# Streaming hybrid-attention step on one core: in the attention loop TensorE weighs the values of an older unit before it multiplies the next unit's scores

## What is computed

```python
s = einsum('bqkgd,bskd->bkgqs', q * d ** -0.5, k)       # scores
s = where(ok, s - slope[h] * distance, -inf)            # ALiBi and mask
p = softmax(concatenate([s, s_meta, sink], -1), -1)     # the sink in A alone
out = einsum('bkgqs,bskd->bqkgd', p, v)                 # weighs the values
```

## Time and profile before

| | |
|---|---|
| median of 3 runs | 1902.87 us (1902.35 to 1903.76) |
| the profiled execution | 1903.1 us |
| its span, first to last instruction | 1901.3 us |
| around the span | 1.8 us |
| granted TensorE clock | 0.998 of full speed |
| PE busy | 1879.1 us, 99% |
| PEld busy | 1778.6 us, 94% |
| DVE busy | 1136.7 us, 60% |
| ACT busy | 712.9 us, 37% |
| POOL busy | 611.2 us, 32% |

### The profile page before, as it was taken

How to read it: one execution, slowest core, us unless ns; L and a number is a source line. 1 busy time by engine, 2 the same in 40 slices (tenths; PEclk the granted TensorE clock), 3 DMA queues, 4 the chain that set the end, 5 groups by cost and what they waited for, 6 DMA issues and landing times.

```text
span 1901.3 us, 32833 instructions
## 1 busy us (share of the span) xinstructions
PE 1879.1 (99%) x11892; PEld 1778.6 (94%) x11892; DVE 1136.7 (60%) x2694; ACT 712.9 (37%) x1424; POOL 611.2 (32%) x493
## 2 busy tenths in 40 slices
PE   9999999999999999999999999999999999999997
PEld 8899999877778999999998889999999999999996
DVE  5259999999765667676664553333333333333336
ACT  5345554233345556555673442222222222222222
POOL 4225554134344334444341022222222222222223
PEclk9999999999999999999999999999999999999999
DMA  6433333233556444444323331111111111111114
GB/s 205 116 84 85 99 95 94 83 107 91 124 134 144 102 102 102 102 102 91 68 69 126 114 126 45 45 44 44 44 44 44 44 44 44 44 44 44 44 44 144
DMA packets 180398, 160.26 MB, mean 84 GB/s; under 512 B 101472, under 2 KB 148432, under 8 KB 180288
## 3 DMA queue, kind: packets, MB, share of 16 engines
q1 hardware_dynamic: 164816, 139.72, 25.9%
q10 hardware_dynamic: 15472, 19.09, 4.4%
HBM read 120.63 MB, written 39.27 MB: 84 GB/s over the span
## 4 chain that ended last, share of the span: by engine, by line
PE 93%; DVE 2%; DMA 0%; issue 0%; SPq 0%; ACT 0%; DVEq 0%
PE ps L1084 23%; PE ps L1906 20%; PE ps L2472 19%; PE ps L1806 11%; PE ps L1782 6%; PE ps L1764 5%; PE ps L2153 5%; PE ps L1056 2%; PE ps L2134 0%; PE ps L2000 0%; DVE y L2416 0%; PE ps L1111 0%; DVE probs L1692 0%; DMA m_in<-merged_scr 0%; DVE total L2396 0%
## 5 line engine op out<-in xcount | busy, mean ns | idle before, releaser
L2472 PE MATMUL ps<-hid_hi,weights 128*128 128x362 f32 (+1 forms) x1536 | 380.3, 327 | 0.0
L1906 PE MATMUL ps<-x2T_hi,weights 128*128 128x362 f32 (+1 forms) x1536 | 378.0, 326 | 0.0
L1906 PEld LDWEIGHTS ps<-x2T_hi,weights 128*128 128x128 f32 x1536 | 272.1, 188 | 0.1
L2396 DVE TENSOR_TENSOR total<-total,ps 128x362 f32<-128x362 f32 (+1 forms) x360 | 189.2, 532 | 138.5 <-PE ps L2472 138.5
L2472 PEld LDWEIGHTS ps<-hid_hi,weights 128*128 128x128 f32 x1536 | 270.4, 188 | 0.0
L1906 PE MATMUL ps<-x2T_lo,weights 128*128 128x362 f32 (+1 forms) x768 | 251.4, 327 | 0.0
L2472 PE MATMUL ps<-hid_lo,weights 128*128 128x362 f32 (+1 forms) x768 | 250.2, 326 | 0.0
L1084 PE MATMUL ps<-xT_hi,w 128*128 128x362 f32 (+1 forms) x960 | 246.1, 330 | 1.6 <-PEq L181 1.6
L2381 DVE TENSOR_TENSOR hidden<-hidden 128x362 f32<-128x362 f32 (+1 forms) x96 | 51.5, 537 | 293.5 <-ACT hidden L2356 293.5
L1893 POOL TENSOR_TENSOR weights<-down_raw,weights 128x512 fp32r<-128x512 f32 x64 | 83.8, 1312 | 380.6 <-ACT weights L1887 380.6
L1035 DVE MATCH_REPLACE8 score<-top,score 128x1024 f32<-128x1024 f32 (+5 forms) x208 | 199.3, 967 | 0.0
(11 more groups left out here) (200 smaller groups left out, 3332.8 us busy)
## 6 DMA issues: line engine op xcount, KB each, us to landing
q_raw<-q_scr SPq DMA_DIRECT2D x80, 256.0 KB, 5.0
w_raw<-in_w_in ACTq DMA_DIRECT2D x64, 256.0 KB, 3.0
up_raw<-in_w_up SPq DMA_DIRECT2D x64, 256.0 KB, 2.8
down_raw<-in_w_down SPq DMA_DIRECT2D x64, 256.0 KB, 2.6
gates<-gate_scr SPq DMA_DIRECT2D x34, 256.0 KB, 4.5
x_in<-in_x_prompt SPq DMA_DIRECT2D x16, 512.0 KB, 5.2
gate_scr<-stage SPq DMA_DIRECT2D x32, 256.0 KB, 3.1
q_scr<-stage SPq DMA_DIRECT2D x40, 181.0 KB, 3.1
```

The lines of the kernel that those rows point to most:

```text
L1906: last = pe.matmul(ps[:, bank, 0:n], a[:, k, fs], b, start=(k == 0 and i == 0), stop=(k == KT - 1 and i == 2))
L2396: dve.tensor_tensor(out, out, more, ALU.add).then_inc(added, 1)
L2472: more = pe.matmul(ps[:, falling_bank(g, final), 0:n], a[:, f, cols], h, start=(f == 0 and i == 0), stop=(f == FT - 1 and i == 2))
```

## The change

Two statements of the step loop change places. In step u TensorE now does turn(u-2), weigh_values(u-3), score(u+1). Nothing else is edited.

```diff
                 if u == UNITS + 1:
                     pe.wait_ge(topped, CHUNK_BASE[UNITS])
                     mix.turn(pe, 0)
+                if u >= 3 and u - 3 < UNITS:
+                    weigh_values(u - 3)
                 if u + 1 < UNITS:
                     score(u + 1)
                 if u == 0:
                     last_group.multiply(pe)
-                if u >= 3 and u - 3 < UNITS:
-                    weigh_values(u - 3)
```

## The result

The changed kernel takes 1948.93 us in the median of four runs (1935.71 to 1952.72); the kernel before, on the same chips, 1902.93 us (1902.35 to 1903.76). The ratio is 1.023, with a 95% interval of 1.0189 to 1.0272: slower, by 46 us. The spread of the four runs goes with their granted TensorE clock: 1935.71 us at 0.998 of full speed, and 1947.66, 1950.20 and 1952.72 us at 0.989, 0.988 and 0.986. The profiled execution is the last of these, 1952.7 us.

A forecast was written before the change was run, and what follows sets the result against it. Attention was taken as bound by TensorE's issue, with section A within a hair of a chain through DVE. 1903.1 + 11.0 (seams) + 21.6 (chain) = 1935.7, so 1935.5 us; range 1914 to 1948, the forecast itself 1929 to 1942.

The forecast's parts named there:

- Part 1, the seams: Changeovers between TensorE's groups in attention steps: the new order costs 11 us more, between 0 and 15.
- W to S: Seam from weighing to scores on TensorE: first wide scores matmul ends 0.26 us after weighing, bounded below by 0.21.
- free seams: Every weight load hidden whatever stands before it, seams cost 0 us; with the chain also covered, 1903 us, chance 0.03.
- Part 2, the chain: Mainly sections A: weighing waits for scores, subtraction, normalising and copy, 0.69 us in each quad; 21.6 us, bounds 0 and 38.
- the link of 0.55 us: DVE's normalising within the chain; the quad's other odd unit lacks it, has 1.30 us and waits 0.14.
- today's waits, 3.8 us: Weighing waits already in the old order, taken off 25.4: 1.8 us in sections A, some 2.0 in the first two sections.
- The sum of both: Whole kernel: 1903.1 + 11.0 + 21.6 = 1935.7, given as 1935.5 us; forecast chance 0.72.
- the clock stays at full speed: Expected of the changed profile: TensorE's clock unchanged while attention is longer by 33 us.
- the wait spreads: Rival: late weighing delays turn and ACT's copy, even units wait too, 13 to 20 us on top, about 1950; chance 0.12.

The follow-up runs named there:

- The run with 76 steps: Old order, but values weighed first in 76 steps inside sections B of pairs 2 and later, against the kernel before: 1907.38 us, ratio 1.0024.
- old order in the first pair: Changed kernel with the old order restored in the first 32 of 268 steps (blocks 15 and 0): 1932.95 us.
- A alone: Kernel before, with values weighed first only in steps whose weighed unit is of attention A: 1922.82 us, ratio 1.0106.
- B alone: Kernel before, with values weighed first only in steps whose weighed unit is of attention B: 1934.28 us.
- the first pair alone: Kernel before, with values weighed first only in the 32 steps of the first pair of blocks: 1924.34 us.
- copies first in A: Changed kernel with DVE copying before it subtracts, only where both units are of attention A: median 1940.42 us.
- old order in eight steps: Changed kernel with the old order in the eight steps weighing units 24 to 31, end of the first section B: 1935.22 us, ratio 1.0176.
- the copy before the normalising: Changed kernel with DVE copying turned tiles before it normalises a quad, subtraction still ahead of the copy: 1919.29 us, ratio 1.0091.
- the old order with the copy before: Kernel before, TensorE order kept, with DVE's copy put before the normalising: 1902.40 us, ratio 1.0002.
- copies first everywhere: DVE copies units of one group before subtracting, in all sections: 1931.96 us on the changed kernel, 1940.85 us on the kernel before.

## Why the prediction was right, and where not

**Where TensorE stands.** That attention is bound by TensorE's issue and that section A is close to a chain through DVE was right, and it was read from the windows and from 3.48 us per quad, not from the page. DVE's share of a section A fell as said, from 94% to 76%: 14.15 of 18.50 us, between 743 and 761.5 us of the changed kernel.

**Part 1, the seams.** W to S was the one seam without a row. The value taken, 0.26 us for 456 keys, is 0.25 in the changed trace, so of the two ends it lies near the upper one. The run with 76 steps measured 4.6 us, some 3.6 of it seams, for 3.7. For all 268 steps the 11 us are thus borne out in kind and about in size; they were not measured as a whole. The count of steps was a little off: 112 wide, 124 of 208 keys and 32 narrower ones, not 128 and 28, which changes 0.1 us. The 141 ns taken for the weight loads of the turns is a median over loads of different widths; those of 128 columns take 155 ns in the mean, still less than the 190 of a product, so the argument keeps its direction. The rule of the Trainium skill ("TensorE: Matmul & The Clock Gate", "Part 2: What happens when you issue a matmul") that was weighed there holds only with the limit that the prediction put to it; with free seams that run would have stood at 1902, or at 1903 with the two waits, below the 1904.8 to 1908.6 us that its interval gives.

**Part 2, the chain.** 1.53 us were forecast and 1.54 measured, 0.69 and 0.14 of wait against 0.71 and 0.16, 4.35 us for a quad against 4.39. The run with the link of 0.55 us taken out gave 1919.3 for 1920. What was subtracted for today's waits, 3.8 us, is less sure: with the old order and these waits gone the time stayed the same. The reasoning that no link can be overtaken, since both engines run in order, was what carried it.

**The sum of both** was 1935.5 us. The only run of the changed kernel at full clock took 1935.71, and with the long stretch at the low clock kept away by eight steps it is 1935.2 for 1934.7 expected.

**What failed.** The step that failed is the sentence "the clock stays at full speed". The median is 1948.93 us, 13.4 above the forecast value and 0.9 above the upper end of the range. The prediction had a rival near that figure, "the wait spreads", 1950 us, but for a reason that did not occur: even units do not wait for ACT, their weighings stand unhindered at 748.46 and 750.38 of the changed kernel. The right number there would have been for a wrong cause. The term to add was the clock: the new order was priced by its seams and waits only, and a lower clock was put at nothing without a reason. In the changed kernel's profiled execution some 41 us at 0.5, and 3 us before, go with 17 us against the run at full clock (1952.7 less 1935.7). The trace puts them in one place: from the last scores of one pair of blocks to those of the next, the second pair takes 19.2 us longer than before, and 4.1 us longer in the kernel with the old order in the first pair, whose clock did not fall; each later pair is the same in these two kernels within 0.1 us. So 15 of the 17 us lie in the stretch at half clock. And the place can't be found by the size of the waits: waits of 0.71 us stand in the later sections A too, and the runs with values first in A alone, or everywhere but in the first pair, kept their clock in all eight runs.

**What of the clock is shown, and what is open.** Shown: in the changed kernel the order of the eight steps near 600 to 617 us decides whether the clock stays low for some 40 us. The kernels that keep the new order there unmended (the changed one, B alone, the first pair alone, copies first in A) fell below 0.992 in 19 of 23 runs; those with the old order there or with the shorter chain (A alone, old order in the first pair, old order in eight steps, the copy before the normalising, inside B, and the old order with the copy before) in none of 37. The list leaves out the two kernels with copies first everywhere: with the old order all four runs stood at 0.995 or 0.996, with the changed order three at 0.996 and one at 0.986. Open: what in these steps does it. The wait of 0.9 us is a suspect, since the clock fell within a microsecond of it in three profiled executions. Against it as the only cause stands the fourth, the second profile of the changed kernel:

```profile
613.00:614.00 1.00, 1.00 (x9) 0.86 (x8) 0.00 (x0) 0.00 (x0) 0.00 (x0) 0.93 0.00 0
614.00:615.00 1.00, 1.00 (x6) 0.82 (x5) 0.87 (x5) 0.36 (x1) 0.89 (x1) 0.50 0.00 0
```

There the clock falls at about 613.9 us, in a row of short groups that TensorE issued without a gap, before the late weighing. And the old order of the eight steps changes more than this wait, so a rival, the short groups themselves, stands untested. Why it then stays low for some 40 us, while TensorE is busy all the time, is open as well.

## What to carry to other kernels

When two groups of an in-order engine change places, follow for each what the other engines wait for, with the ends of each link from the trace, and set that chain against what the engine has to do in the meantime: here a chain of 1.85 us had 1.76 us of cover and was left with 1.16. A page that shows an engine at 99% does not say whether a wait is near, so look at the pace of one period and at the windows of its helpers. A new order must also be asked what it does to the clock, and with a kernel whose runs spread, the runs belong to be sorted by their granted clock before anything is explained.

## What the runs showed of the hardware that was not expected

- The granted clock can fall to its lower level, 1.2 GHz, in a kernel in which TensorE is busy for some 98% of the span. It fell at the same place, 613 to 617 us, in four profiled executions of three kernels, and stayed low for about 37 to 51 us in which the clock was 0.50 and TensorE went on with its matmuls. The Trainium skill ("TensorE: Matmul & The Clock Gate", "Part 1: The HAM clock gate (the "warmup" mystery)") has the clock rise again with activity; the row for 615 to 660 us shows the lower level with TensorE busy for 44.32 of 45 us, and the rise only near 658. Falls of some 3 us, at other places, stand in seven profiled executions.
- The low clock cost less than half of its length, in three profiled executions held against the run of the same kernel at full clock: 17 us for 44, 14 us for 37.5 (1949.71 less 1935.71) and 23 us for 55 (B alone, 1938.82 less 1916.12). The matmuls of the 45 us point the same way: 199 in place of 330, so 0.60 of the pace and not 0.5. Why was not followed up.
- A weight load for a transposing matmul is shorter than one of the same width for a product. In attention of the kernel before (busy us, mean ns of one), with 190 ns for those of the scores:

```profile
L1782 PEld LDWEIGHTS ps<-ident,probs 128*128 128x128 f32 x696 | 88.3, 155 | 4.8
```

- The first matmul of a group costs more or less by what stands before it: scores of 456 keys 0.25 us after a weighing and 0.21 after a turn. That the lengths of the weight loads set this difference was the reasoning of the prediction; no run tests it by itself.
